# Differential attention: another order of its projection pieces, an earlier rotation of q, and attention units one quarter earlier

## What is computed

```
qkv = h @ w_qkv
q, k, v = split(qkv, 3)
q = rmsnorm(q per map of 64) * q_gain ; k = rmsnorm(k per map of 64) * k_gain
q, k = rotate the first 16 dimensions of each map by the position
p = softmax(causal(q k^T / sqrt(64)))          for each of the 16 maps
a = p[map 0] - lam * p[map 1]                   for each of the 8 heads
o = rmsnorm(a @ v) * subln * (1 - lambda_init) ; out = o @ w_out
```

## Time and profile before

| | |
|---|---|
| median of 3 runs | 2256.24 us (2254.52 to 2257.69) |
| the profiled execution: its own time | 2251.79 us |
| its span, first to last instruction | 2250.0 us |
| TensorE busy | 95% of the span |
| VectorE, ScalarE, GpSimd busy | 78%, 64%, 3% |
| mean granted TensorE clock | 0.977 of full speed |

### The profile page before, as it was taken

One profiled execution on the slowest core, in us unless ns is written; L12 is line 12 of the kernel. 1 busy time (PEld: TensorE's weight loads), 2 busy tenths in 40 slices (PEclk: granted clock), 3 DMA queues, 4 the chain that ended last, 5 costly groups with the idle time before them and its releaser, 6 DMA issues.

```text
span 2250.0 us, 31466 instructions
## 1 busy us (share of the span) xinstructions
PE 2126.9 (95%) x9970; PEld 1721.1 (76%) x9970; DVE 1746.7 (78%) x2351; ACT 1434.6 (64%) x1928; POOL 63.1 (3%) x66
## 2 busy tenths in 40 slices
PE   8998998998997999999997999999999999999998
PEld 7975776875776887887774787878788787878786
DVE  4655898755988756545775898989898998989897
ACT  5662775453775644444542787878787887878785
POOL 0000000000000000111110000000000000000000
PEclk9998999998999999999997999999999999999999
DMA  6225784233873446542330998989799898989895
GB/s 253 113 76 236 303 330 189 107 142 139 367 315 123 170 176 256 212 181 89 122 113 1 405 377 323 372 321 380 313 380 372 328 373 321 377 320 376 317 384 206
DMA packets 81400, 577.11 MB, mean 256 GB/s; under 512 B 9392, under 2 KB 9392, under 8 KB 12848
## 3 DMA queue, kind: packets, MB, share of 16 engines
q1 hardware_dynamic: 79744, 570.40, 64.5%
q0 software_dynamic: 1584, 5.77, 0.7%
HBM read 575.08 MB, written 1.05 MB: 256 GB/s over the span
## 4 chain that ended last, share of the span: by engine, by line
PE 78%; DVE 11%; issue 5%; ACT 4%; DMA 1%; DVEq 0%; POOL 0%; SPq 0%; ACTq 0%; POOLq 0%
PE bank L480 22%; PE bank L482 22%; PE bank L481 21%; PE bank L940 2%; DVE h L1772 1%; PE bank L1413 1%; PE bank L1379 1%; DVE gu_lo L1720 1%; PE bank L604 1%; PE bank L2808 1%; DVE dn_lo L1720 1%; DVE pj_lo L517 1%; DVE small L376 1%; ACT gu_hi L1548 1%; ACT dn_hi L1556 1%
## 5 line engine op out<-in xcount | busy, mean ns | idle before, releaser
L1720 DVE TENSOR_TENSOR gu_lo<-ffw_gu,gu_hi 128x1024 fp32r<-128x1024 f32 x620 | 754.1, 1236 | 89.3 <-ACT gu_hi L1548 74.6
L1548 ACT CAST gu_hi<-ffw_gu 128x1024 fp32r<-128x1024 f32 x620 | 648.0, 1052 | 101.7 <-PE bank L482 69.2
L480 PE MATMUL bank<-gu_hi,xg_lo 128*128 128x512 f32 x1152 | 462.7, 402 | 5.8 <-DVE xg_lo L1720 4.7
L482 PE MATMUL bank<-gu_hi,xg_hi 128*128 128x512 f32 x1152 | 452.4, 393 | 0.0
L481 PE MATMUL bank<-gu_lo,xg_hi 128*128 128x512 f32 x1152 | 451.6, 392 | 0.0
L1720 DVE TENSOR_TENSOR dn_lo<-ffw_d,dn_hi 128x1024 fp32r<-128x1024 f32 x299 | 365.0, 1230 | 57.0 <-ACT dn_hi L1556 47.8
L1556 ACT CAST dn_hi<-ffw_d 128x1024 fp32r<-128x1024 f32 x310 | 325.2, 1055 | 95.0 <-PE bank L482 91.3
L480 PE MATMUL bank<-dn_hi,hidt_lo 128*128 128x512 f32 x664 | 265.1, 399 | 28.6 <-DVE hidt_lo L1720 28.6
L482 PE MATMUL bank<-dn_hi,hidt_hi 128*128 128x512 f32 x664 | 259.3, 391 | 0.0
L481 PE MATMUL bank<-dn_lo,hidt_hi 128*128 128x512 f32 x664 | 259.2, 390 | 0.0
L480 PEld LDWEIGHTS bank<-gu_hi,xg_lo 128*128 128x128 f32 x1152 | 217.7, 189 | 49.2 <-DVE xg_lo L1720 5.3
(11 more groups left out here) (410 smaller groups left out, 2774.8 us busy)
## 6 DMA issues: line engine op xcount, KB each, us to landing
ffw_gu<-in_gate_up_m SPq DMA_DIRECT2D x288, 1024.0 KB, 6.9
ffw_d<-in_down_m SPq DMA_DIRECT2D x144, 1024.0 KB, 7.6
pieces<-in_pieces SPq DMA_DIRECT2D x70, 1024.0 KB, 7.0
ffw_gu<-in_gate_up_ff SPq DMA_DIRECT2D x22, 1024.0 KB, 6.9
ffw_d<-in_down_ff SPq DMA_DIRECT2D x11, 1024.0 KB, 8.9
pieces<-in_pieces SPq DMA_DIRECT2D x4, 512.0 KB, 8.1
norm_vec<-in_ln_g POOLq DMA_DIRECT2D x4, 512.0 KB, 4.0
norm_vec<-in_ln_b POOLq DMA_DIRECT2D x4, 512.0 KB, 4.9
```

The lines of the kernel that those rows point to most:

```text
L480: nc.tensor.matmul(bank, a_lo, b_hi, start=start, stop=False)
L482: return nc.tensor.matmul(bank, a_hi, b_hi, start=False, stop=stop)
L1548: nc.scalar.copy(gu_hi[:, 2 * k:2 * k + 2, :], ffw_gu[:, blk["slot"], 2 * k:2 * k + 2, :])\
L1720: return V.tensor_tensor(out, x, hi.bitcast(F32), ALU.subtract)
```

## The change

1. The pieces come in the order k, q, v for the first half of the heads and again for the second half (before: q, k, v). The piece list, `DA_MAPS` and the order in which GpSimd answers the roots (`roots_in`) follow.
2. The turns of the four q and k pieces stand behind the quarters 7, 10, 20 and 22 (before: 6, 11, 20 and 23). Step i of the first eight units stands behind quarter 11 + i (before: 12 + i).
3. VectorE: for k, the sums are in quarter 0 of the next piece, and the multiplication by the root with the rotation in quarter 1, both as before. For q, the rotation comes first, in quarter 0, and waits only for ScalarE's copies; the sums are in quarter 1, behind that quarter's `pj_lo`; the wait for the root and the logit scale are in quarter 2, ahead of VectorE's copy of the turned piece. The end of the output norm goes from quarter 22 to 21, ahead of the sums of q.

```
-    da = [(("q", "k", "v")[i // 2], "tok", columns("l1_da_w_qkv_2", 512 * i, 512 * (i + 1)), 512) for i in (0, 2, 4, 1, 3, 5)]
+    da = [(("q", "k", "v")[i // 2], "tok", columns("l1_da_w_qkv_2", 512 * i, 512 * (i + 1)), 512) for i in (2, 0, 4, 3, 1, 5)]
...
-                    5: by_tile, 6: [*((da_ms[n], da_ms[n]) for n in (0, 2, 1, 3)), *((da_hs_flat[k], da_hs_flat[k]) for k in range(2)), *by_tile], 7: []}
+                    5: by_tile, 6: [*((x, x) for x in (da_ms[2], da_ms[0], da_ms[3], da_hs_flat[0], da_ms[1], da_hs_flat[1])), *by_tile], 7: []}
...
-    DA_MAPS = (0, 2, 1, 3)
-    da_asked = {}
-    DA_TURN = {6: 0, 11: 1, 20: 2, 23: 3}
-    DA_STEP = {12 + i: i for i in range(10)}
+    DA_MAPS = (2, 0, 3, 1)
+    DA_TURN = {7: 0, 10: 1, 20: 2, 22: 3}
+    DA_STEP = {11 + i: i for i in range(10)}
...
+    def da_logit_scale_vector(n):
+
+        root_wait_vector()
+        ms = da_ms[DA_MAPS[DA_ROUND[n]]]
+        vlink(V.tensor_scalar(ms, ms, -HD ** -0.5, None, ALU.mult))
...
-                if k == 0 and n - 1 in DA_ROUND:
-                    da_heads_begin_vector(dve, n - 1)
+                after = da_pieces[n - 1][0] if n else None
+                if after == "k" and k == 0:
+                    da_sums_vector(dve, n - 1)
                 piece_lo_vector(dve, "da", n + 1, (k,))
                 if i >= 2:
                     da_write_vector(dve, i - 2)
+                if after == "k" and k == 1:
+                    da_keys_vector(n - 1)
+                    da_rotate_vector(n - 1)
+                if after == "q" and k == 0:
+                    read_wait(dve, "da", 0, n)
+                    read_wait(dve, "da", 1, n)
+                    da_rotate_vector(n - 1)
                 if i == 9:
                     da_norm_begin_vector(0)
-                if k == 1 and n - 1 in DA_ROUND:
-                    da_heads_end_vector(dve, n - 1)
-                if at == 22:
+                if at == 21:
                     da_norm_end_vector(0)
+                if after == "q" and k == 1:
+                    da_sums_vector(dve, n - 1)
+                if after == "q" and k == 2:
+                    da_logit_scale_vector(n - 1)
                 if at in DA_TURN:
                     da_turned_vector(dve, DA_TURN[at])
```

More of the change, by code:

```diff
@@ L2921, in da_scalar, with da_sums_vector @@
         first_weights_scalar(act, "m2")
-    def da_heads_begin_vector(dve, n):
+    def da_sums_vector(dve, n):
         o = DA_ROUND[n]
@@ L2931, in da_heads_begin_vector, with da_keys_vector, da_rotate_vector @@
         root_ask_vector()
-        da_asked[n] = roots["asked"]
-    def da_heads_end_vector(dve, n):
-        m = DA_MAPS[DA_ROUND[n]]
[L2937 to L2949, removed]
+    def da_logit_scale_vector(n):
+        root_wait_vector()
+        ms = da_ms[DA_MAPS[DA_ROUND[n]]]
+        vlink(V.tensor_scalar(ms, ms, -HD ** -0.5, None, ALU.mult))
+    def da_keys_vector(n):
+        root_wait_vector()
+        m = DA_MAPS[DA_ROUND[n]]
+        for j in range(T):
+            vlink(V.scalar_tensor_tensor(out=da_qk[:, j, 8 * m:8 * m + 8, :],
+                                         in0=psum[2 * (n % 2) + j].rearrange("p (m d) -> p m d", d=HD),
+                                         scalar=rstd[:, j:j + 1], in1=over(da_ms[m][:, 8 * j:8 * j + 8], 2, HD),
+                                         op0=ALU.mult, op1=ALU.mult), sem(f"bank{j}_read"))
+    def da_rotate_vector(n):
+        m = DA_MAPS[DA_ROUND[n]]
+        x = da_qk[:, :, 8 * m:8 * m + 8, 0:ROT]
         cos, sin = over(da_cos[:, m // 2], 2, 8), over(da_sin[:, m // 2], 2, 8)
```

## The result

The changed kernel takes 2263.49 us, median of 8 runs (2261.52 to 2265.98), against 2256.18 (2254.52 to 2257.69, 8 runs): 7.3 us slower. The ratio estimated from all executions is 1.0038, 95% interval 1.0028 to 1.0048; the two medians alone give 1.0032. The forecast was 2262.2 us, 6.0 slower.

What follows compares the result with a forecast made beforehand. TensorE was followed as the bound, busy all 35.00 us from 1112 to 1147. Terms -1.1 - 0.4 + 2.5 + 1.5 + 1.9 = +4.4, plus 1.6 for the clock, made 2256.24 + 6.0 = 2262.2 us; range 2254.8 to 2267.5.

Steps and rivals of the forecast that it cites:

- First turn: TensorE's wait ahead of the first turned piece: 1.25 us instead of 2.38, counted as -1.1 us.
- Second turn: TensorE's wait of 0.44 us ahead of the second turned piece, behind quarter 10, goes: counted as -0.4 us.
- Logits of unit 0: TensorE waits about 2.5 us for VectorE's copy of the turned q, where before there was none: +2.5 us.
- Transposes of unit 7: Last unit of the first half: VectorE's list between masks grows to 11.7 us, TensorE waits 1.5: +1.5 us.
- Logits of unit 8: In the tail, TensorE waits 2.9 us for the copy of the last turned q; part of the tail's +1.9 us.
- Fourth turn and mix turn: TensorE's waits of 0.27 and 0.57 us before these turns in the tail were to be none.
- the wait ahead of that product: TensorE, ready at 15.2, waits 1.45 us ahead of the first output product at 16.7; before, 1.04.
- The clock: TensorE's clock falls to half speed behind one of the two long new waits: +1.6 us; range 0 to 3.2.
- Rival 1: Waits as computed, but the clock stays or one wait is smaller: +2.5 to +4.5 us; chance 0.34.
- Rival 2: VectorE meets each root already answered, so the long waits vanish: -3.5 us, 2252.7; chance 0.08.
- Rival 3: VectorE's copy holds nobody up because TensorE's quarters wait for `pj_lo`: -1 to +1 us, 2256; chance 0.08.
- Rival 4: GpSimd and VectorE conflict, so roots beside `pj_lo` take longer: given nothing but the range; changes no chance.

Runs made afterwards that it cites:

- experiment 1: Changed kernel with VectorE's copy of the turned q ahead of its wait for the root and the logit scale, in quarters 10 and 22: 2255.15 us.
- experiment 5: Changed kernel with q's sums back in quarter 0, behind the rotation, copy still behind the root; norm end waits for its own root alone: 2255.74 us.
- Experiment 4: Changed kernel with the first units put back, step i behind quarter 12 + i: 2262.51 us.
- experiment 2: Changed kernel with VectorE's copy of the turned q ahead of the root's wait in quarter 22 only: 2258.78 us.
- experiment 3: Changed kernel with six unused float32 matmuls of 512 columns on TensorE between the mix turn and the logits of unit 8: 2258.26 us.
- experiment 6: Changed kernel with the rotation of the second k one quarter behind its keys, in quarter 18 instead of 17: 2260.99 us.
- experiment 7: Changed kernel with copies before root waits, second q's sums before the norm's end, first turn behind quarter 8, second k's rotation a quarter later: 2252.15 us.

## Why the prediction was right

**The waits were right one by one.** First turn: 1.25 predicted, 1.26 measured. Second turn: none and none. Logits of unit 0: 2.5, 2.58. Transposes of unit 7: 1.5, 1.50, with 11.71 us between the two masks for 11.7. Logits of unit 8: 2.9, 2.75. Fourth turn and mix turn: none and none. The tail's two times are right to 0.05 us: 14.55 from the start of output 7 (1154.27) to the logits of unit 8, 14.5 predicted, and 16.73 to the first output product, 16.7 predicted. Only the wait ahead of that product was off, 1.45 against 0.56: VectorE's copies of the mix turn release it, ending at 1170.90, 0.10 before it, while the slow clock had stretched the logits in front of it (0.56 between their starts; 0.22 in experiment 1, ahead of its fall) and so filled part of the wait. The sum up to there was 4.4 for 4.73 measured; the 0.3 between them is not assigned to a term.

**The cause of the two long waits is the one named**: the root of q is asked one quarter later than before, and VectorE's wait for it stands ahead of the copy that TensorE needs. Experiments 1 (another order) and 5 (an earlier question) each remove the wait ahead of unit 8 and shrink the one ahead of unit 0 from 2.58 to 0.64 and 1.44, by two independent edits. Experiment 4 shows that the earlier unit 0 is a second condition for the first wait, and none for the last.

**The clock was the term mis-sized.** The prediction took one fall at 1.6 us. There was one new one, in the tail, and behind the first output product it cost 2.3, since it lasted through 6.5 us, not through eight matmuls. With 2.3 the sum would have been 6.7; measured 7.3. The reason that I gave for choosing one, the second pair of waits being above 3.26 together, is not shown: experiments 1 and 2 have the pair in one wait of 2.73, and the clock fell too. That exactly one of the two waits was followed by a fall was therefore a lucky choice; with none or two of 2.3 the forecast would have been 2260.6 or 2265.2. The prediction also took the size from the start of the phase alone and said that no row shows a fall behind a wait of this size between matmuls. The trace of before had one that none of its rows shows, in the same phase, behind waits of 2.06 and 0.99:

```profile
1193.37 1.23 PE L2801 MATMUL bank<-ident,arena 128*128 128x128 f32 x8 [2.06 <-DVEq L296]
...
1194.50:1201.30 6.80, 5.81 (x8) 2.52 (x8) 5.49 (x6) 2.73 (x3) 0.00 (x0) 0.50 0.00 0
```

The kernel before takes 19.75 us from that mix turn to the router, and 16.91 in experiment 3, where the clock held: 2.8 us for a fall of this length. That would have been the nearer price, and have raised the forecast to 2263.4.

**The rivals.** Rival 1 (inside 4.5 us) nearly holds for the waits alone, 4.73; the clock took the time clearly over the line. Rival 2 (roots covered) needed a fast GpSimd; its sixteen-wide roots took 2.90 each time but the first. Its price was also wrong: with the waits of 2.5 and 2.9 gone and the 1.45 at 0.9, the prediction's own terms add to about -1.6 us, not -3.5, and with a root of 1.63 to about +1.9, not +0.9. Rival 3 (TensorE late on its own account) is excluded: TensorE waits for `pj_lo` once, 0.8 us, as before. Rival 4 (GpSimd and VectorE disturb one another, by the Trainium skill's "Advanced Engine Details and Errata", section "GPSIMD Details"): the root that ran beside `pj_lo` and the one that ran while VectorE idled both took 2.90, so nothing of it is seen here. The rule of the clock, from the Trainium skill's "TensorE: Matmul & The Clock Gate", section "What's actually happening", agrees with experiment 3, where unused matmuls in the wait kept the clock up. What the prediction drew from it, a slow stretch behind both new waits, did not come true: behind the 2.58 us the clock stayed at 1.00.

## What to carry to other kernels

When a dependency is loosened (q need not wait for its root), look at where the rest of it lands: the wait did not go, it moved to the place in the in-order queue where something urgent was standing behind it. Ask for slow answers first and wait for them last, behind every operation that others need. And price an idle stretch of TensorE at its length plus what the clock may take behind it, which for the wait of 2.75 us was 2.3 more.

## What was not expected of the hardware

Behind a wait of 2.58 us ahead of the logits of unit 0 the clock stayed at 1.00 in all four versions that had it (changed, experiments 2, 3 and 6); behind waits of 2.73 to 4.68 in the tail it fell to 0.50 in all five that had them (changed, experiments 1, 2, 4 and 6). Length alone may not be what tells them apart: the first lies between dense quarters of projection, the second between short transposes and logits. No run separates the two.

A slow stretch can also be absent where the same waits stand: at the second mix turn the waits are 2.06 and 0.9 to 1.0 in experiments 3 and 7 alike, and the stretch behind them was at 1.00 in experiment 3 and slow in 7:

```profile
1193.00:1200.00 7.00, 5.87 (x13) 3.24 (x14) 5.74 (x7) 3.88 (x4) 0.00 (x0) 0.54 0.01 2
```

These are one execution each, and executions of the same kernel differ by as much: that of experiment 3 took 2252.13 us at a mean granted clock of 0.980 and 2261.25 at 0.973, the kernel before 2247.86 at 0.979 and 2259.46 at 0.974. So a version's time has a part of some us that goes with the clock. Whether an edit elsewhere switches it or it comes and goes by itself the runs do not separate, and a profile has to be read for it before a difference of this size is put down to an edit.
